# Half-row gate matmuls in pairs, and a recurrence whose second group of heads keeps its tokens in the other half of the partitions

## The reference, cut to what matters

```python
r = jax.nn.sigmoid(jnp.einsum("bshi,hij->bshj", xh, gate_a_w).reshape(b, s, D_RNN) + gate_a_b)
ig = jax.nn.sigmoid(jnp.einsum("bshi,hij->bshj", xh, gate_x_w).reshape(b, s, D_RNN) + gate_x_b)
```

```python
def step(state, inp):
    r_t, w_t, k_t, v_t, a_t, b_t = inp
    sa = jnp.einsum('bhij,bhj->bhi', state, a_t)
    state = state * w_t[:, :, None, :] + sa[..., None] * b_t[:, :, None, :] + v_t[..., None] * k_t[:, :, None, :]
    return state, jnp.einsum('bhij,bhj->bhi', state, r_t)
```

## Time and profile before

| | |
|---|---|
| median of 3 runs | 3629.59 us |
| profiled execution, own time | 3631.98 us |
| its span | 3630.2 us |
| PE busy | 96% of the span |
| DVE, ScalarE, POOL busy | 50%, 32%, 13% |
| mean granted clock of TensorE | 0.985 |

### The profile page before, as it was taken

How to read it: one execution, slowest core, us unless ns; L and a number is a source line. 1 busy time by engine, 2 the same in 40 slices (tenths; PEclk the granted TensorE clock), 3 DMA queues, 4 the chain that set the end, 5 groups by cost and what they waited for, 6 DMA issues and landing times. The chain is left out here.

```text
span 3630.2 us, 52790 instructions
## 1 busy us (share of the span) xinstructions
PE 3498.9 (96%) x22046; PEld 2874.0 (79%) x22046; DVE 1819.1 (50%) x2092; ACT 1151.4 (32%) x1356; POOL 480.0 (13%) x436
## 2 busy tenths in 40 slices
PE   6999999999999999999999999999999998999998
PEld 5578888888888888886688888887778996768886
DVE  7655243453435553436653345554785554455342
ACT  3632123432222231223532233233652222332122
POOL 1111011020110020111011012000340110111011
PEclk9999999999999999999999999999999998999998
DMA  3223232233232333233133223333222114213231
GB/s 125 61 87 104 93 102 95 82 97 100 93 104 86 101 93 104 93 102 99 45 106 104 93 93 105 111 122 99 87 72 63 33 39 153 82 51 100 93 104 58
DMA packets 314090, 329.62 MB, mean 91 GB/s; under 512 B 22834, under 2 KB 305461, under 8 KB 313397
## 3 DMA queue, kind: packets, MB, share of 16 engines
q1 hardware_dynamic: 307141, 303.39, 26.4%
q0 software_dynamic: 4464, 19.40, 1.6%
q10 hardware_dynamic: 2304, 4.20, 0.3%
HBM read 312.28 MB, written 14.68 MB: 90 GB/s over the span
## 5 line engine op out<-in xcount | busy, mean ns | idle before, releaser
L478 PE MATMUL ps<-xh,wh 128*128 128x512 f32 x2360 | 936.2, 397 | 26.8 <-DVE wl L419 23.4
L478 PE MATMUL ps<-xl,wh 128*128 128x512 f32 x2360 | 923.0, 391 | 0.0
L478 PE MATMUL ps<-xh,wl 128*128 128x512 f32 x2360 | 922.6, 391 | 0.0
L419 DVE TENSOR_TENSOR wl<-raw,wh 128x2048 fp32r<-128x2048 f32 (+2 forms) x287 | 642.5, 2239 | 461.9 <-ACT wh L414 461.4
L414 ACT ACTIVATE wh<-raw 128x2048 fp32r<-128x2048 f32 (+2 forms) x287 | 527.1, 1837 | 712.9 <-PE ps L478 678.1
L478 PEld LDWEIGHTS ps<-xh,wh 128*128 128x128 f32 x2360 | 446.1, 189 | 134.7 <-issue 38.3
L478 PEld LDWEIGHTS ps<-xl,wh 128*128 128x128 f32 x2360 | 446.2, 189 | 97.1 <-issue 5.5
L478 PEld LDWEIGHTS ps<-xh,wl 128*128 128x128 f32 x2360 | 445.6, 189 | 93.8
L478 PE MATMUL ps<-hh,wh 128*128 128x512 f32 x1280 | 498.3, 389 | 1.1 <-DVE wl L419 0.8
L478 PE MATMUL ps<-hl,wh 128*128 128x512 f32 x1280 | 498.0, 389 | 0.0
L478 PE MATMUL ps<-hh,wl 128*128 128x512 f32 x1280 | 498.0, 389 | 0.0
(11 more groups left out here) (410 smaller groups left out, 3766.7 us busy)
## 6 DMA issues: line engine op xcount, KB each, us to landing
raw<-in_mlp_w SPq DMA_DIRECT2D x128, 1024.0 KB, 5.2
raw<-in_ffn_w SPq DMA_DIRECT2D x32, 1024.0 KB, 5.4
raw<-in_w_in SPq DMA_DIRECT2D x31, 1024.0 KB, 5.3
raw<-in_a_w_in SPq DMA_DIRECT2D x20, 1024.0 KB, 5.1
raw<-in_c_w_in SPq DMA_DIRECT2D x12, 1024.0 KB, 5.1
raw<-in_a_w_out SPq DMA_DIRECT2D x16, 640.0 KB, 4.1
raw<-in_b_w_in SPq DMA_DIRECT2D x8, 1024.0 KB, 5.3
raw<-in_xa_wkv SPq DMA_DIRECT2D x8, 1024.0 KB, 5.3
```

Of the source, the lines that this page charges most:

```text
L419: nc.vector.tensor_tensor(wl[:, p.slot(su), 0:n], raw[:, p.slot(su), 0:n], wh[:, p.slot(su), 0:n], ALU.subtract).then_inc(lower, 1)
L478: last = nc.tensor.matmul(banks[mt][:, 0:st.n], wt[at_, slot, k, mt * P:mt * P + P], ops[oi][at_, kk, 0:st.n], start=k == 0 and su == 0 an ...
```

## The change

**Gate stage.** Of an off-diagonal block only the rows that the straddling head needs are multiplied: for i = o + 1 the first 64 rows (`low`), for i = o - 1 the last 64 (`high`). The order for a tile is: low part of gate 0 and high part of gate 1, then the full blocks of both gates, then high part of gate 0 and low part of gate 1. The last ones wait on a semaphore (`a_halves`) for the first ones.

**Recurrence.** `chan` gives the half of a head's channel-indexed rows, as before; `toks` gives the half of its token-indexed rows, for group 1 the opposite one. `together` issues several kinds of matmul in turn, for i = 0..3 and both h. The identity is put into the first TM (`TI`, in `hf`), so that DVE copies the first X. Z is accumulated in its PSUM banks, which it keeps through the levels, and ScalarE copies it to SBUF after each level instead of DVE's addition. X and Y share a bank per group. Group 1 runs half a level behind group 0. The turns, the first product and the K turn of chunk c + 1 are issued in levels 1, 4 and 5 of chunk c; the second product stands between the two halves of U. Output and state parts on different row halves of the same bank are separated by a wait on `ck_crossed`. DVE updates the state after the first X of the next chunk. Head sums go to both halves of 8 columns, the spread to two banks. The waits on the spills of chunk 0 move to ScalarE's turns in level 1 and to DVE's mask in level 4.

**Elsewhere.** Some semaphores are merged: the SGU bias counts with its matrix, layer 2's y with layer 1's, the memory tokens with x; their readers wait for both.

Of the functions that are rewritten whole, the added lines and their context are shown here (the lines removed are in the functions above).

```diff
-    Vt, Bt, Kt, TM = ([at(f"c{n_}{i_}", 2 * k_ + (12, 8)[i_], [P, NH2, CH], base_at=(XH_AT, XT_AT)[i_]) for i_ in range(2)]
-                      for k_, n_ in enumerate(["Vt", "Bt", "Kt", "TM"]))
+    VB = [at(f"cVB{i_}", (12, 8)[i_], [P, 2, NH2, CH], base_at=(XH_AT, XT_AT)[i_]) for i_ in range(2)]
+    Vt, Bt = ([VB[i_][:, e] for i_ in range(2)] for e in range(2))
+    Kt, TM = ([at(f"c{n_}{i_}", 2 * k_ + (16, 12)[i_], [P, NH2, CH], base_at=(XH_AT, XT_AT)[i_]) for i_ in range(2)]
+              for k_, n_ in enumerate(["Kt", "TM"]))
+    TI = hf[:, 0].rearrange("p (q n) -> p q n", n=CH)
...
-            mine = [(b, i) for b, (i, oo) in enumerate(BAND) if oo == o]
-            for g in range(2):
-                for m, (b, i) in enumerate(mine):
-                    last = nc.tensor.matmul(ps[4 + 2 * (t % 2) + g][:], gw[:, b, g], xc[:, 5 * grp + i],
-                                            start=m == 0, stop=m == len(mine) - 1)
+            full, low, high = ([(b, i) for b, (i, oo) in enumerate(BAND) if oo == o and i - o == e] for e in (0, 1, -1))
+            LO, HI, ALL = slice(0, 64), slice(64, P), slice(0, P)
+            first = [(rows_, b, i, g) for g in range(2) for rows_, part in ((LO, low), (HI, high))[g:g + 1] for b, i in part]
+            last_ = [(rows_, b, i, g) for g in range(2) for rows_, part in ((HI, high), (LO, low))[g:g + 1] for b, i in part]
+            middle = [(ALL, b, i, g) for g in range(2) for b, i in full]
+            seq = first + middle + last_
+            for m, (rows_, b, i, g) in enumerate(seq):
+                mine = [n_ for n_, e in enumerate(seq) if e[3] == g]
+                if m == len(first) + len(middle):
+                    pe.wait_ge(s("a_halves"), done(l) + t + 1)
+                last = nc.tensor.matmul(ps[4 + 2 * (t % 2) + g][:], gw[rows_, b, g], xc[rows_, 5 * grp + i],
+                                        start=m == mine[0], stop=m == mine[-1])
+                if m == len(first) - 1:
+                    last.then_inc(s("a_halves"), 1)
...
-            sp.wait_ge(s("ck_turned"), 3 * c + 3)
+            sp.wait_ge(s("ck_kprod"), c + 1)
...
+    PB = (0, 1)
+    YX, ZB = (4, 5), (6, 2)
+    WB = (7, 3)
...
+    def chan(h, q):
+
+        return HP[h]
+
+    def toks(h, q):
+
+        return HP[h] if q < 4 else HP[1 - h]
+
+    def together(*fns):
+
+
+        for i in range(4):
+            last = [[fn(h, i) for h in range(2)][-1] for fn in fns]
         return last
...
+    def group(g, fn):
+
+        return lambda h, i: fn(h, 4 * g + i)
...
+        def turn(src, eye, at_):
+            return lambda h, q: mm(ps[banks[q // 4]][toks(h, q), at_ * 256 + q % 4 * CH:at_ * 256 + q % 4 * CH + CH],
+                                   src(h, q), eye[chan(h, q), :], start=True, stop=True)
+        for e in srcs_:
+            last = together(group(0, turn(*e)), group(1, turn(*e)))
+        last[-1].then_inc(s("ck_turned"), 1)
...
+        def product(h, q):
+            k = chan(h, q)
+            return mm(ps[PB[q // 4]][toks(h, q), q % 4 * P:q % 4 * P + P], (BT, KT)[which][k, c, q],
+                      AR[k, c, q].rearrange("p a n -> p (a n)"), start=True, stop=True)
+        together(group(0, product), group(1, product))[-1].then_inc(s(done), 1)
...
+        pe_products(pe, 0, 0, "ck_bprod")
+        pe_turn(pe, 0, 0, YX)
+        pe_turn(pe, 0, 1, WB)
+        pe.wait_ge(s("ck_bmasked"), 1)
+        pe_products(pe, 0, 1, "ck_kprod")
         for c in range(NC):
             b = c % 2
+            more = c < NC - 1
+
+            first_x = lambda h, q: mm(ps[YX[q // 4]][toks(h, q), cols(q)], TI[toks(h, q), q], i64[toks(h, q), :], start=True, stop=True)
+            first_z = lambda h, q: mm(ps[ZB[q // 4]][chan(h, q), cols(q)], i64[toks(h, q), :], TI[toks(h, q), q], start=q % 4 == 0, stop=True, skip_group_check=True)
+            more_x = lambda h, q: mm(ps[YX[q // 4]][toks(h, q), cols(q)], Z[chan(h, q), q], Yt[chan(h, q), q], start=True, stop=True)
+            more_z = lambda h, q: mm(ps[ZB[q // 4]][chan(h, q), cols(q)], Yt[chan(h, q), q], Z[chan(h, q), q],
+                                     start=False, stop=True, skip_group_check=True)
+            w0_tok = lambda h, q: mm(ps[WB[q // 4]][chan(h, q), cols(q)], TLK[b][toks(h, q), q, 0], Vt[b][toks(h, q), q],
+                                     start=q % 4 == 0, stop=False, skip_group_check=True)
+            w0_state = lambda h, q: mm(ps[WB[q // 4]][chan(h, q), cols(q)], AR[chan(h, q), c, q, 0], ST[chan(h, q), q],
+                                       start=False, stop=True, skip_group_check=True)
+            u_of = lambda h, q: mm(ps[YX[q // 4]][toks(h, q), cols(q)], Z[chan(h, q), q], W0[chan(h, q), q], start=True, stop=True)
+            ds_b = lambda h, q: mm(ps[WB[q // 4]][chan(h, q), cols(q)], Bt[b][toks(h, q), q], U[toks(h, q), q], start=q % 4 == 0, stop=False, skip_group_check=True)
+            ds_k = lambda h, q: mm(ps[WB[q // 4]][chan(h, q), cols(q)], Kt[b][toks(h, q), q], Vt[b][toks(h, q), q],
+                                   start=False, stop=True, skip_group_check=True)
+            o_v = lambda h, q: mm(ps[ZB[q // 4]][chan(h, q), cols(q)], Vt[b][toks(h, q), q], TLK[b][toks(h, q), q, 1],
+                                  start=q % 4 == 0, stop=False, skip_group_check=True)
+            o_u = lambda h, q: mm(ps[ZB[q // 4]][chan(h, q), cols(q)], U[toks(h, q), q], TLB[b][toks(h, q), q, 1],
+                                  start=False, stop=False, skip_group_check=True)
+            o_state = lambda h, q: mm(ps[ZB[q // 4]][chan(h, q), cols(q)], ST[chan(h, q), q], AR[chan(h, q), c, q, 1],
+                                      start=False, stop=True, skip_group_check=True)
+
+            pe.wait_ge(s("ck_turned_copied"), 4 * c + 4)
+            pe.wait_ge(s("ck_tm"), 6 * c + 1)
             for g in range(2):
+                together(group(g, first_x))[0].then_inc(s(f"ck_xm{g}"), 1)
+            if c:
+                pe.wait_ge(s("ck_out"), c)
+            last = together(group(0, first_z), group(1, first_z))
+            last[0].then_inc(s("ck_zm0"), 1)
+            last[1].then_inc(s("ck_zm1"), 1)
+
             for l in range(1, 6):
+                times = lambda h, q: mm(ps[YX[q // 4]][chan(h, q), cols(q)], TM[l % 2][toks(h, q), q], X[toks(h, q), q],
+                                        start=True, stop=True)
+                pe.wait_ge(s("ck_x0"), 5 * c + l)
+                pe.wait_ge(s("ck_tm"), 6 * c + l + 1)
+                together(group(0, times))[0].then_inc(s("ck_y0"), 1)
+                if l > 1:
+                    pe.wait_ge(s("ck_y_copied1"), 5 * c + l - 1)
+                    pe.wait_ge(s("ck_z1"), 6 * c + l - 1)
+                    last = together(group(1, more_x), group(1, more_z))
+                    last[0].then_inc(s("ck_xm1"), 1)
+                    last[1].then_inc(s("ck_zm1"), 1)
+                if l == 1 and more:
+                    pe.wait_ge(s("ck_kmasked"), c + 1)
+                    pe_turn(pe, c + 1, 0, PB)
+                if l == 2:
                     if c:
+                        if more:
+                            pe.wait_ge(s("ck_turned_copied"), 4 * c + 6)
+                        pe_head_sums(pe, c - 1)
                         pe.wait_ge(s("ck_state"), c)
+                    pe.wait_ge(s("ck_kmasked"), c + 1)
+                    together(group(0, w0_tok), group(1, w0_tok))[1].then_inc(s("ck_crossed"), 1)
+                if l == 3:
+                    together(group(0, w0_state))[0].then_inc(s("ck_w0"), 1)
+                    pe.wait_ge(s("ck_crossed"), 2 * c + 1)
+                    together(group(1, w0_state))[0].then_inc(s("ck_w0"), 1)
+                    if c:
+                        pe_head_spread(pe, c - 1)
+                if l == 4 and more:
+                    pe.wait_ge(s("ck_turned_copied"), 4 * c + 6)
+                    if c:
+                        pe.wait_ge(s("hd_scaled"), 2 * c)
+                    pe_products(pe, c + 1, 0, "ck_bprod")
+                if l == 5 and more:
                     pe.wait_ge(s("ck_w0_copied"), 2 * c + 2)
+                    pe_turn(pe, c + 1, 1, WB)
+                pe.wait_ge(s("ck_y_copied0"), 5 * c + l)
+                pe.wait_ge(s("ck_z0"), 6 * c + l)
+                if l < 5:
+                    together(group(0, more_x))[0].then_inc(s("ck_xm0"), 1)
+                pe.wait_ge(s("ck_x1"), 5 * c + l)
+                last = together(group(0, more_z), group(1, times))
+                last[0].then_inc(s("ck_zm0"), 1)
+                last[1].then_inc(s("ck_y1"), 1)
+            pe.wait_ge(s("ck_y_copied1"), 5 * c + 5)
+            pe.wait_ge(s("ck_z1"), 6 * c + 5)
+            together(group(1, more_z))[0].then_inc(s("ck_zm1"), 1)
             pe.wait_ge(s("ck_w0_copied"), 2 * c + 2)
+            pe.wait_ge(s("ck_z0"), 6 * c + 6)
+            together(group(0, u_of))[0].then_inc(s("ck_u"), 1)
+            if more:
+                pe.wait_ge(s("ck_bmasked"), c + 2)
```

(116 more changed lines are left out.)

193 lines of the change are left out of this document (36 added, 157 removed).

## The result

The changed kernel took 3600.1 us (median of 4 runs, 3599.78 to 3604.14), the kernel before 3628.8 us beside it (4 runs, 3627.19 to 3629.70): ratio 0.992, 95% interval 0.991 to 0.993. It is faster, by 28.7 us where 83 were forecast. The time lies inside the range, at its upper end, and outside the likeliest case's own range (3528 to 3570).

The account below looks back on a forecast made before the run. The PE was taken to bound gate stages and recurrence. Profiled 3632.0 - 15.6 (gates) - 74 (recurrence) + 6 (instruction delivery) = 3548.4; the median of runs lies 2.4 lower: 3546 us, range 3528 to 3606.

Parts of the forecast that it names:

- likeliest case: Recurrence: 16 matmuls together on all four quarters run at full rate; own range 3528 to 3570 us, chance 0.65.
- Gates: Gate stage: half-row pairs run together, then ScalarE is late next; its roots start 7.8 us earlier, twice: -15.6 us.
- The price of a four: Recurrence: 16 matmuls (32 records) together on all four quarters take 0.467 us; bounds 0.467 and 0.933.
- first rival: Recurrence: PE starts records at a limited rate, 0.70 or 0.80 us per 32 records; 3581 or 3595 us, chance 0.19.
- No drains: Recurrence: denies the rival that each change between quarters costs 0.09 us, run about 3738 us, chance 0.05.
- fours of use: Recurrence: denies the rival that 16 matmuls on four quarters take 0.933 us, gaining nothing; about 3617 us, chance 0.11.
- the clock as before: Recurrence: denies that more pauses bring a half-clock spell each chunk, 3 us each, up to 3570 us; no chance given.
- The ring: Recurrence, one level of group 0: Y, copy, X, add take 2.36 us against 1.87 of PE work; 1.1 lost in four levels.
- instruction delivery: Recurrence: PE waits for its instructions, asked for 1.4 times as often per us; 0.75 us a chunk, +6 (0 to 14).

Follow-up runs that it names:

- one_pass: Changed kernel with the recurrence's matmul operands read as bfloat16, two instructions a matmul instead of four (head sums and spread excepted): 3497.47 us, ratio 0.9638 to the kernel before.
- both_fewer: Changed kernel with 128 matmuls and 151 PE waits fewer, slices as they were: 3590.24 us against 3630.76 for the kernel before, ratio 0.9885.
- half_cols: Changed kernel with moving operands of the ring, W0, U, state and output cut from 64 to 32 columns, as many instructions: 3610.45 us.
- rec_only: Changed kernel with the old order of the gate matmuls put back: 3613.26 us against 3628.14 for the kernel before, ratio 0.9956.

## Why the prediction was wrong, step by step

**Gates: right.** Roots forecast at 139.0, seen at 139.76; the pairs, the step of 7.75 us on ScalarE and the PE's wait on wl (5.12) came as described. A middle tile takes the PE 3.84 us (98.59 to 102.43) and not 3.6, which ScalarE's pace hides. Forecast -15.6; measured -15.4 by the start of the recurrence in the profiles, -15.3 alone.

**The price of a four: right.** 0.467 us forecast, 0.51 to 0.52 measured in the rows above for the starts of 32 records, and 0.466 at the least in the stretch. The work by starts is 157 us, and eight chunks of 19.5 are 156. This also settles the first rival: a limit on starts would have shown as 0.70 or 0.80 a four, and the rows show 16 ns from record to record over four quarters. The Trainium skill (TensorE: Matmul & The Clock Gate, "Wait — 56ns, not 53.3ns?") has start-to-start never below about 25 ns, which by an estimate from it would be 0.80 us for a four: the measurement decides against it here.

**No drains, fours of use, the clock as before: right.** L1805 starts right behind L1775's 32 records though the quarters change; the work by starts fell by 74 us; the mean clock of the stretch is 0.98 as before.

**The ring: not the bound.** The waits on cYt come to 4.7 us in all and those on cX to 1.4, 0.8 a chunk together, where over 3 would have been the sign of a wrong ring. The pauses that don't end on issue are 32 us, 31 before. one_pass ran the same ring in 18.3 us a chunk.

**The failed step** is the term "instruction delivery ... I take 0.75 a chunk, +6 (0 to 14)". Measured are 46 us of waits on issue, 5.8 a chunk; with the end of the last record before each, the pauses on issue are 59 us. That is 53 more than the 6 of the sum, and it is the whole miss: the recurrence was forecast at 264.5 - 74 + 6 = 196.5 us and took 247.9. The prediction's own sign for this, PE idle on issue for more than 1 us a chunk, came true. The PE's busy time of 190 us is no second miss: a record lasts 0.22 us, and 157 us of starts with one such end at each of 172 pauses are about 190.

I had taken one stall of 1.22 us (the trace of before has a second, of 0.67) and scaled it with the rate of demand. Delivery doesn't grow like that. While the work took 31.5 us a chunk, 7.4 blocks that can come every 3.37 us (25) were hidden under it and left two marks. At a work of 22 they no longer fit. What was to be had from the trace of before is the instruction queue's 59 packets in 264.5 us and their smallest distance, 3.37 us: with the changed kernel's 7.6 blocks a chunk, 7.6 x 3.37 = 25.6 us at the least, 2.8 more than the 22.85 forecast, and about 3568 by the same sum. That estimate would have been nearer and still 32 us short, as the blocks came every 4.06 us and not every 3.37. That the chunk takes 30 and not 26 is explained in part: without the slices' transfers it took 0.4 to 1.5 us less, and with 663 instructions fewer (both_fewer) 28.8.

**The range held by luck.** Its upper part, 3565 to 3606, was there for a limit on starts, which the rows refute. In the likeliest case the sum with delivery at its bound of 14 gives 3554, and its own range ended at 3570.

What is shown: the lost time stands at the borders of instruction blocks, and each such pause ends 1.2 to 1.6 us after a block's packet; the columns (half_cols) and the copies (one_pass) don't bound the chunk. What stays open: why two blocks are never under 3.2 us apart though a packet is on the queue for about 1 us, and 4.9 with the increments; whether memory or the PE's sequencer sets it was not told apart. Also open is why the same recurrence took 239, 243 and 248 us in three profiles; the clock spell ahead of it goes with a shorter one in rec_only and was not tested.

## What to carry to other kernels

Before forecasting that an engine will do more per microsecond, count its instructions: divide the stretch by the packets of the instruction queue, compare the result with their smallest distance, and treat that as a resource of its own that a faster array runs into. Then number the engine's instructions and see whether its waits on issue stand a multiple of a block apart. A small float32 matmul is four instructions here (two matmul records, two weight loads), and the instructions come at 13 to 16 ns each (a block in 3.3 to 4.06 us). So 64x64 work on four quarters wants fewer and wider matmuls and few stand-alone increments on PE; leaving out satisfied waits and spreading the transfers gave 9 and 7 us, each near what runs differ. A small mark of a resource in a profile tells that it is near its limit, and not what it will cost beyond it.

## What the runs showed of the hardware that was not expected

With an increment of a semaphore ahead of every fourth matmul the recurrence took 0.139 us longer for each, half of it as waits on issue and much of the rest at the lower clock; a satisfied wait cost 0.02 to 0.06 us. Blocks of 256 instructions never came closer than 3.2 us in any of these kernels. Wherever the PE had waited over 0.3 us for a block, it went on 1.2 to 1.6 us after the end of a packet. A four of 64x64 matmuls took 0.49 us with 32 columns and 0.51 with 64. The granted clock fell to 0.52 in a stretch with half the instructions and fewer columns, and that kernel was faster than the changed one by 102 us all the same.
